# Moving the top-k rounds of the last sparse-attention block from twelve attention units into the first three

## The reference, cut to what matters

```python
score = jnp.einsum('bqhk,bqh->bqk', rel, w_blk.astype(jnp.float32))
score = jnp.where(key_pos[None, None, :] <= qpos[None, :, None], score, -jnp.inf)
_, idx = lax.top_k(score, top_k)
```

## Time and profile before

| | |
|---|---|
| median of the runs | 4223.11 us |
| time of the profiled execution | 4224.37 us |
| its span in the profile | 4222.6 us |
| PE busy | 3936.5 us (93%) |
| PEld busy | 2507.2 us (59%) |
| DVE busy | 1600.5 us (38%) |
| ACT busy | 849.1 us (20%) |
| POOL busy | 748.7 us (18%) |
| MAX8 of line 3017 | 96 instructions, 53.9 us |
| MATCH_REPLACE8 of line 3019 | 96 instructions, 52.2 us |

### The profile page before, as it was taken

How to read it: one execution, slowest core, us unless ns; L and a number is a source line. 1 busy time by engine, 2 the same in 40 slices (tenths; PEclk the granted TensorE clock), 3 DMA queues, 4 the chain that set the end, 5 groups by cost and what they waited for, 6 DMA issues and landing times.

```text
span 4222.6 us, 93974 instructions
## 1 busy us (share of the span) xinstructions
PE 3936.5 (93%) x40148; PEld 2507.2 (59%) x40148; DVE 1600.5 (38%) x3343; ACT 849.1 (20%) x1847; POOL 748.7 (18%) x617
## 2 busy tenths in 40 slices
PE   5999999989988888888999999999999999999998
PEld 4544444445557777777444443447588864657887
DVE  1413113145444545444131122345245424525363
ACT  2200000020035555554110001116000001330000
POOL 4100000000033333443000000000234410013343
PEclk8999999999999999999999999999999999999999
DMA  8377888871300000000359998120122211102221
GB/s 343 126 305 287 332 335 309 314 290 57 119 7 13 12 12 13 12 12 12 128 250 428 429 428 358 46 75 1 60 80 97 83 68 60 41 21 80 86 94 40
DMA packets 54204, 619.13 MB, mean 147 GB/s; under 512 B 5648, under 2 KB 8976, under 8 KB 18320
## 3 DMA queue, kind: packets, MB, share of 16 engines
q1 hardware_dynamic: 49664, 599.41, 36.0%
q10 hardware_dynamic: 2448, 9.05, 0.6%
q0 software_dynamic: 1792, 6.29, 0.5%
HBM read 602.40 MB, written 12.32 MB: 146 GB/s over the span
## 4 chain that ended last, share of the span: by engine, by line
PE 81%; DMA 6%; issue 5%; DVE 5%; ACT 1%; DVEq 1%; PEld 0%; SPq 0%; POOL 0%; ACTq 0%; PEldq 0%; POOLq 0%
PE bank L908 62%; PE bank L1389 13%; DMA ring<-slabs 3%; DMA work<-slabs 3%; PE bank L1773 1%; PE bank L936 1%; PE bank L1781 1%; PE bank L1790 1%; DVE work L2790 1%; DVE hx L2485 0%; PE bank L1779 0%; PE bank L1440 0%; PE bank L1776 0%; DVE work L2470 0%; PEld bank L908 0%
## 5 line engine op out<-in xcount | busy, mean ns | idle before, releaser
L908 PE MATMUL bank<-ring,work 128*32 128x256 f32 (+3 forms) x7002 | 764.1, 439 | 72.2 <-DMA ring<-slabs 60.1
L908 PE MATMUL bank<-work 128*128 128x256 f32 (+8 forms) x3590 | 762.9, 422 | 13.3 <-DVE work L3154 5.7
L908 PEld LDWEIGHTS bank<-work 128*128 128x128 f32 (+3 forms) x3590 | 483.1, 179 | 282.8 <-issue 211.8
L908 PEld LDWEIGHTS bank<-ring,work 128*32 128x32 f32 (+2 forms) x7002 | 317.2, 124 | 494.2 <-issue 388.0
L908 PE MATMUL bank<-hx,ring 128*128 128x512 f32 (+1 forms) x1344 | 484.3, 514 | 4.8 <-DVE hx L2485 2.8
L908 PE MATMUL bank<-work,ring 128*128 128x256 f32 (+1 forms) x1616 | 477.6, 454 | 6.8 <-DVE work L2732 3.4
L908 PEld LDWEIGHTS bank<-work,ring 128*128 128x128 f32 x1616 | 305.6, 190 | 173.0 <-issue 132.4
L908 PEld LDWEIGHTS bank<-hx,ring 128*128 128x128 f32 x1344 | 253.5, 190 | 223.5 <-issue 201.5
L1389 PE MATMUL bank<-work 64*64 64x64 f32 x11520 | 322.6, 225 | 65.1 <-issue 51.4
L3334 POOL TENSOR_TENSOR work<-ring 128x512 f32<-128x512 f32 (+1 forms) x44 | 69.3, 1575 | 1621.1 <-ACT work L2002 1222.6
L1389 PEld LDWEIGHTS bank<-work 64*64 64x64 f32 x11520 | 289.6, 137 | 91.2 <-issue 88.2
(11 more groups left out here) (326 smaller groups left out, 4832.7 us busy)
## 6 DMA issues: line engine op xcount, KB each, us to landing
ring<-slabs SPq DMA_DIRECT2D x228, 2048.0 KB, 9.9
work<-slabs SPq DMA_DIRECT2D x48, 2048.0 KB, 18.3
work<-kv SPq DMA_DIRECT2D x18, 384.0 KB, 3.1
kv<-work SPq DMA_DIRECT2D x2, 3072.0 KB, 15.8
kv<-work ACTq DMA_DIRECT2D x6, 512.0 KB, 17.7
work<-tabs ACTq DMA_DIRECT2D x1, 2176.0 KB, 8.6
resx<-xT SPq DMA_DIRECT2D x1, 2048.0 KB, 11.1
outT<-hx ACTq DMA_DIRECT2D x8, 256.0 KB, 2.1
```

Source lines behind the costliest of these rows:

```text
L908: return pe.matmul(out, lhsT, rhs, start=(k == 0), stop=(k == n - 1))
```

## The change

In units 0, 1 and 2 two rounds of block 3 now follow red(u+1,1) and two more follow red(u+1,3), so that each of these units has four rounds. Units 3 to 11 have none any more. The number of rounds stays 12 (3 units of 4, in place of 12 units of 1). The mask ("keep", 3) is made after ev(3) in place of ev(12). No other engine's list is changed.

```diff
-    AT_DVE += [("red", _u + 1, _h) for _h in range(HEADS)] * _more + [("ev", _u)] + [("keep", 3)] * (_u == 12)
+    AT_DVE += [("red", _u + 1, _h) for _h in range(HEADS)] * _more + [("ev", _u)] + [("keep", 3)] * (_u == 3)
...
                         if u + 1 < len(ATTENTION):
                             lowest(u + 1, h)
-                        if u < 12 and h == 1:
-                            rounds(3, 1)
+                        if u < 3 and h % 2:
+                            rounds(3, 2)
                     rows_out(u)
-                    if u == 12:
+                    if u == 3:
                         hidden(3)
```

## The result

The changed kernel took 4247.05 us (median of four runs, 4244.70 to 4250.39), the kernel before on the same chip 4221.82 us (4216.38 to 4224.37). The ratio is 1.0062, with a 95% interval of 1.0044 to 1.0080. The change costs about 25 us. I had forecast 18 more and a range that ended at 4247, so the sign was right, the size too small, and the time lies outside the range by 0.05 us, which is far less than the scatter of the runs.

What follows compares the result with a forecast made beforehand. PE was taken as the bound (busy 109.65 of 110.20 us in the first layer's units). 4224.37 + 14.6 for waits + 3.4 for the clock = 4242.4, less 1.3 to the median: 4241 us, range 4232 to 4247.

Steps and rivals of the forecast that it cites:

- The waits: PE waits 3.6, 1.5 and 2.2 us before OT(0), OT(1), OT(2): 7.3 us a layer, 14.6 for two.
- rivals 1 and 4: 1: only first wait real, 4233 us, chance 0.09; 4: rounds wait for something else, run later, 0.02 with unseen gains.
- the step from ev to OT: From the start of an ev that PE waits for to OT: 0.83 us in the trace, taken as 0.7.
- The removed rounds: Nine rounds of units 3 to 11 removed: gain 0, bounds 0 and 0.5 us a layer.
- The mask: Mask moved to after ev(3), fitting in DVE's idle 1.06 us before red(5,0): cost 0, bounds 0 and 0.7.
- The clock: PE's granted clock may fall after the new waits: 3.4 us for both layers, bounds 0 and 10.2.
- The price of one short stretch: A 3.4 us stretch at half clock loses 1.7 us of PE's work; 1.3 after the first wait.
- The count: Clock falls among units 0 to 2: one or two a layer likeliest, put at 1.7 us a layer.
- the length: Each low stretch of PE's clock after a new wait was taken to last 3.4 us.
- Units 3 to 15 should each take as long as before to within 0.1: Sign expected in the profile after: behind units 0 to 2 the delay stays at 7.3 us a layer.
- The second rival: Every new wait takes PE's clock down: six times 1.7 us in place of 3.4, 4248 us, chance 0.09.

Runs made afterwards that it cites:

- warm2: Changed kernel with 3, 1 and 2 products that nothing reads filling PE's waits ahead of OT(0), OT(1) and OT(2): 4233.90 us against 4221.34, ratio 1.0029.
- norounds: Kernel without the twelve rounds among the units, mask still made after ev(3): 4224.20 us against 4218.97 for the kernel before, ratio 1.0012.
- unit2only: Against the kernel before: four rounds in unit 2, none in units 0 and 1, one each in units 3 to 10: 4233.66 us against 4221.34, ratio 1.0037.
- warm_first2: Changed kernel with unread products (3 and 1) ahead of OT(0) and OT(1) alone, third wait left empty: 4247.55 us against 4223.85, ratio 1.0058.
- warm_third: Changed kernel with two unread products ahead of OT(2) alone, first two waits left empty: 4244.20 us against 4221.34, ratio 1.0060.
- spread6: Against the kernel before: two rounds in each of units 0 to 5, mask after ev(6): 4229.10 us against 4218.97, ratio 1.0027.
- evfirst: Changed kernel with the second pair of rounds of units 0, 1 and 2 moved behind ev(u): 4231.32 us against 4221.34, ratio 1.0030.

## Why the prediction was half right

**The waits: right.** The prediction named three waits of line 1808 on ev in each layer and a delay that grows as 3.6, 5.1, 7.3. All three came, released by DVE line 3047, and DVE's rounds ran without a gap, so the prediction's rivals 1 and 4 fall. With the clock kept up (warm2) it grows as 3.3, 4.6, 6.7. The 14.6 us of the sum measured 13.6. At OT(0) the forecast was 0.25 us too late, and half of that is the step from ev to OT, taken as 0.7 us: after the change ev(0) starts at 2846.03 and OT(0) at 2846.60, so it was 0.57. With the waits left empty the second one was 0.88 us and not 1.5, since PE at the low clock came to it later.

**The removed rounds: right.** A gain of 0 was taken, and norounds shows it from the other side.

**The mask: right.** In the first layer of the profile after, it starts at 2875.55 and the next reduction at 2876.52 still found DVE idle for 0.54 us, released by PE.

**The clock: the term that was mis-sized.** The prediction put 3.4 us for both layers, with an upper bound of 10.2. It measured 10.9 and 17.6 in the units of the two profiles, and 14 to 17 in the times. The price of one short stretch held: "A low stretch of 3.4 us at half clock loses 1.7 us", taken as 1.3 behind the first wait, and OT(1) came 1.4 and 1.6 us later than in warm2. The count was two falls a layer, behind the first wait and the third, where "one or two" were expected and one was priced. With both of 3.4 us, in the first layer of the first profile, they cost 125.4 - 121.9 = 3.5 us.

The step that failed worst is the length. I took the length of every low stretch from the two in the earlier trace rows, both 3.4 us (the window of 3.75 us holds 0.35 at full clock). The runs show 3.4 and 6.8 us behind the first wait, and 3.4 or 13.7 behind the third. A stretch of 13.7 us lost 6.0 us by itself where it can be isolated (unit2only: 8.3 - 2.3; warm_first2: 13.1 - 6.9 = 6.2). It lies in unit 3 and the start of unit 4, where DVE waits for PE, so nothing absorbs it. My upper bound was none, because it multiplied a count by the shortest length seen. With it fell the sign "Units 3 to 15 should each take as long as before to within 0.1": from OT(2) to OT(3) it took 7.5 us before, and 9.2 to 13.0 in the four layers of the changed kernel's profiles. Why a stretch lasts 3.4 us in one execution and 13.7 in another stays open.

What I overlooked stood in the trace of before: it was read only for the units and for two idle times of PE near them. In the units the clock was 1.00 throughout, so there was nothing to see. Two earlier stages of the same kernel were not looked at; there the clock stayed low for 13.7 and 17.1 us in one piece:

```profile
918.60:932.30 13.70, 8.65 (x157) 6.83 (x150) 9.28 (x24) 1.69 (x4) 0.00 (x0) 0.50 1.01 429
2027.90:2045.00 17.10, 17.10 (x86) 9.27 (x86) 3.13 (x10) 0.00 (x0) 0.00 (x0) 0.50 0.01 1
```

The second rival, "every new wait takes the clock down", gave 4248 and comes nearest to the time, but not for its reason: the second wait of a layer, which shrank to 0.88 us, was followed by no low clock in any profile of the changed kernel.

The Trainium skill, in "TensorE: Matmul & The Clock Gate", section "HAM oscillation — how this bites in real kernels", tells of waits of some 3 to 5 us, each of them followed by the low clock. The trace agrees for the waits of that length: behind 3.0 to 3.2 us the clock fell six times of six (the changed kernel and warm_third). Shorter ones that kernel doesn't have. Here, of the eight waits of about 2 us that were left empty, six were followed by the low clock (all four of the changed kernel, one of two in warm_first2, one of two in unit2only), and of those under 0.9 us none.

**The profile against the times.** The profiled executions alone would have misled: 4238.53 against 4224.37 is 14 us, which matches the waits alone and would have looked like a proof that the clock costs nothing. The units' own lengths gave 24.5.

## What to carry to other kernels

An engine with half its time free can still take work only where its free time is: compare, unit by unit, its work with that of the engine that sets the pace, and put in each unit less than the difference (in spread6 PE was 0.9 to 1.3 us late after three units even so). If the pace-setting engine is the matrix engine, price a new wait twice, once for the wait and once for the clock behind it, and for the second look at the longest low stretch anywhere in the trace, not at the shortest. Profile more than one execution: the length of a low stretch differs between them. If a wait can't be avoided, products that nothing reads, sized a little under it, took the second price away here (1.0062 against 1.0029).

## What the runs showed of the hardware

- A granted clock of 0.50 lasted 3.4, 6.8 or 13.7 us behind the waits of this kernel, and the same instructions got different lengths in different executions.
- With the clock at 0.50, PE did 60 matmuls of units 3 and 4 in 13.7 us, where it did 101 in 13.8 us at 1.00.
- Waits of up to 1.5 us in six pieces (evfirst) brought one low stretch of 3.4 us in two layers; waits of 3.0 to 3.2 us brought one six times of six, waits of 1.97 to 2.16 us six times of eight, and in unit2only the wait of 2.16 us didn't while the one of 1.99 did.
- A low stretch of 3.4 us cost 1.4 to 1.6 us (OT(1) of the changed kernel against warm2), one of 13.7 us cost 6.0 to 6.2 (one layer against the other in unit2only and warm_first2).
- DVE, started late, ran reductions, rounds, reciprocal and ev with no idle time that the profile shows, and the costs of single rows added up to within 0.1 us in a unit: red(1,2) to ev(0) was forecast at 4.25 us and took 4.19.
